# Hybrid Hyena / attention / RG-LRU block on one core: VectorE updates x first at the end of an FFN group, unused TensorE products at the norms and in the prologue

## The reference

```python
def rmsnorm(x, g):
    xf = x.astype(jnp.float32)
    y = xf * lax.rsqrt(jnp.mean(xf * xf, axis=-1, keepdims=True) + NORM_EPS)
    return (y * g.astype(jnp.float32)).astype(x.dtype)
...
def swiglu(h, w_in, w_out):
    gate, up = jnp.split(h @ w_in, 2, axis=-1)
    return (jax.nn.silu(gate) * up) @ w_out
...
    for i in range(DEPTH):
...
        m_lat = jnp.split((s_lat @ ada_w[i] + ada_b[i])[:, None, :], 6, axis=-1)
        m_ctx = jnp.split(s_ctx @ ada_w[i] + ada_b[i], 6, axis=-1)
        h_lat = modulate(rmsnorm(x_lat, norm1_g[i]), m_lat[0], m_lat[1])
        h_ctx = modulate(rmsnorm(x_ctx, norm1_g[i]), m_ctx[0], m_ctx[1])
...
        x_lat = x_lat + m_lat[2] * y_lat
        x_lat = x_lat + m_lat[5] * swiglu(modulate(rmsnorm(x_lat, norm2_g[i]), m_lat[3], m_lat[4]),
                                          ffn_w_in[i], ffn_w_out[i])
```

## Time and profile before

| | us |
|---|---|
| median of 3 runs | 3465.39 |
| lowest, highest | 3463.32, 3470.06 |
| the profiled execution | 3466.77 |
| its span, first to last instruction | 3465.0 |
| TensorE busy | 3201.0 |
| VectorE busy | 1670.7 |
| ScalarE busy | 939.8 |
| GpSimd busy | 350.0 |

### The profile page before, as it was taken

How to read it: one execution, slowest core, us unless ns; L and a number is a source line. 1 busy time by engine, 2 the same in 40 slices (tenths; PEclk the granted TensorE clock), 3 DMA queues, 4 the chain that set the end, 5 groups by cost and what they waited for, 6 DMA issues and landing times. The chain is left out here.

```text
span 3465.0 us, 39696 instructions
## 1 busy us (share of the span) xinstructions
PE 3201.0 (92%) x15846; PEld 2539.7 (73%) x15846; DVE 1670.7 (48%) x2146; ACT 939.8 (27%) x1205; POOL 350.0 (10%) x263
## 2 busy tenths in 40 slices
PE   6999997899766989999999999899969899999999
PEld 5788864555455778878888888678757788888887
DVE  5433237566687452444343444767774433333333
ACT  4222223344311231111111111377872311111111
POOL 1000000577422100000000000200001000000000
PEclk9999999799878989999999999999989999999999
DMA  4666610000312201111111111211113111111111
GB/s 188 224 224 207 200 42 1 0 1 9 124 73 85 97 31 37 37 41 38 36 36 36 36 36 38 75 40 37 38 33 115 49 49 43 48 48 48 48 48 73
DMA packets 65195, 231.63 MB, mean 67 GB/s; under 512 B 7911, under 2 KB 17511, under 8 KB 63560
## 3 DMA queue, kind: packets, MB, share of 16 engines
q1 hardware_dynamic: 50600, 199.26, 16.7%
q0 software_dynamic: 4000, 17.37, 1.4%
q10 hardware_dynamic: 10496, 13.63, 1.2%
HBM read 204.55 MB, written 25.69 MB: 66 GB/s over the span
## 5 line engine op out<-in xcount | busy, mean ns | idle before, releaser
L252 PE MATMUL bank<-h_pair,w_hi 128*128 128x512 f32 (+1 forms) x2448 | 620.1, 380 | 8.1 <-DVE h_pair L1849 7.2
L252 PEld LDWEIGHTS bank<-h_pair,w_hi 128*128 128x128 f32 x2448 | 442.3, 188 | 97.2 <-issue 8.9
L238 DVE TENSOR_TENSOR w_lo<-w_raw,w_hi 128x1024 fp32r<-128x1024 f32 x194 | 262.6, 1354 | 433.0 <-ACT w_hi L232 429.3
L268 PE MATMUL bank<-h_pair,w_hi 128*128 128x512 f32 x1344 | 366.8, 394 | 0.0
L252 PE MATMUL bank<-h_pair,w_lo 128*128 128x512 f32 (+1 forms) x1224 | 353.5, 379 | 0.0
L1781 DVE SCALAR_TENSOR_TENSOR x<-bank,c_mods,x 128x1024 f32<-128x1024 f32 (+3 forms) x280 | 273.0, 1007 | 143.5 <-PE bank L252 140.3
L232 ACT ACTIVATE w_hi<-w_raw 128x1024 fp32r<-128x1024 f32 x194 | 203.8, 1050 | 481.6 <-PE bank L268 238.5
L268 PEld LDWEIGHTS bank<-h_pair,w_hi 128*128 128x128 f32 x1344 | 227.9, 188 | 43.4
L252 PEld LDWEIGHTS bank<-h_pair,w_lo 128*128 128x128 f32 x1224 | 221.3, 188 | 44.0
L268 PE MATMUL bank<-h_pair,w_lo 128*128 128x512 f32 x672 | 208.3, 391 | 0.0
L276 DVE COPY ffn_part<-bank 128x256 f32<-128x256 f32 x42 | 17.8, 425 | 383.5 <-PE bank L268 383.5
(11 more groups left out here) (336 smaller groups left out, 5137.5 us busy)
## 6 DMA issues: line engine op xcount, KB each, us to landing
w_raw<-in_weights SPq DMA_DIRECT2D x194, 512.0 KB, 3.3
ada_late_w<-in_ada_w SPq DMA_DIRECT2D x80, 512.0 KB, 3.8
x<-in_x SPq DMA_DIRECT2D x2, 5120.0 KB, 15.7
h_gate<-u_scratch SPq DMA_DIRECT2D x4, 2560.0 KB, 9.3
ada_w<-in_ada_w SPq DMA_DIRECT2D x16, 512.0 KB, 17.4
u_scratch<-uc POOLq DMA_DIRECT2D x12, 640.0 KB, 5.1
spec_lat<-f_spec ACTq DMA_DIRECT2D x4, 1792.0 KB, 9.2
h_spec<-spec_lat SPq DMA_DIRECT2D x2, 3584.0 KB, 12.4
```

Of the source, the lines that this page charges most:

```text
L238: e.tensor_tensor(k.w_lo[s][:, :], k.w[s][:, :], k.w_hi[s][:, :].bitcast(F32), ALU.subtract).then_inc(k.split_lo[s], 1)
L252: mm = e.matmul(out[:, c:c + m], w[:, c1:c1 + P], x[:, c:c + m], start=(first and kk == 0 and n == 0), stop=(last and kk == kt - 1 and n = ...
L268: mm = e.matmul(out[:, c:c + m], w, x[:, half, c:c + m], start=(first and n == 0), stop=(last and n == 2))
```

## The change

In an FFN group VectorE no longer forms the low half of the second hidden tile and the `w_lo` of slot 1 before it updates x. The low half now stands behind x for m = 0, the `split_lo` of slot 1 behind x for m = 1. In the first group, which no take_out follows directly, the low half stays in its place.

Unused products (`spare`: ones times ident, float32, 128 by 128 by 128, written to an accumulator bank that nobody reads before it is written anew) are added: 20 at the end of `even_out`, `ffn(0)` and `rg_out`, behind a wait for x of tile m = 6; 10 behind the spreading of each of the three later norms; 36 in the prologue behind the filter's second layer. In the prologue ones and ident are loaded ahead of x, the first weight pair ahead of the last four adaLN tiles, and ScalarE splits that pair behind tiles 10 and 11.

```diff
+SPARE_FIRST, SPARE_AHEAD, SPARE_BEHIND = 36, 20, 10
+
+def spare(k, e, count, bank=0):
+    for _ in range(count):
+        e.matmul(k.bank[:, bank, 0:P], k.ones[:, :], k.ident[:, :], start=True, stop=True)
+
+def spare_ahead(k, e, ph):
+    e.wait_ge(k.acc_free[0], ph.a0 + ph.uses + 1)
+    spare(k, e, SPARE_AHEAD)
...
@@ Norm.tensor
         self.stats(k, e)
         self.spread(k, e)
+        spare(k, e, SPARE_BEHIND)
...
@@ prologue, sync
+            e.dma_start(k.ones[:, :], d["ones"]).then_inc(ones_landed, 16)
+            e.dma_start(k.ident[:, :], d["ident"]).then_inc(ones_landed, 16)
             e.dma_start(k.x[:, :, :], d["x"]).then_inc(x_landed, 16)
-            ada.load_first(k, e)
-            e.dma_start(k.ones[:, :], d["ones"]).then_inc(ones_landed, 16)
-            e.dma_start(k.ident[:, :], d["ident"]).then_inc(ones_landed, 16)
+            ada.load_first(k, e, 0, 12)
+            load_pair(k, e, w0)
+            ada.load_first(k, e, 12, ADA_FIRST)
             for name in names:
                 e.dma_start(k.c[name][:, :], d[name]).then_inc(others, 16)
-            load_pair(k, e, w0)
...
@@ prologue, tensor
             mm.then_inc(mm_full, 1)
+            e.wait_ge(ones_landed, 32)
+            spare(k, e, SPARE_FIRST, 7)
             e.wait_ge(silu_ready, 1)
...
                 if n == STATS_BEHIND:
-                    e.wait_ge(ones_landed, 32)
                     e.wait_ge(ss_ready, 1)
...
@@ prologue, scalar
-                if n >= ADA_FIRST - 2:
-                    s = n - (ADA_FIRST - 2)
+                if STATS_BEHIND < n <= STATS_BEHIND + 2:
+                    s = n - (STATS_BEHIND + 1)
                     split_hi(k, e, s, w0, k.acc_full[s], 1)
...
@@ even_out, ffn (if not last) and rg_out, tensor, at the end
+            spare_ahead(k, e, ph)
...
@@ ffn, vector
+            def low_half(g, buf, t):
+                e.wait_ge(hi_done, g * HG + (t + 1))
+                e.tensor_tensor(hid_lo[buf][:, t, 0:tokens], hid[:, 0:tokens],
+                                hid_hi[buf][:, t, 0:tokens].bitcast(F32), ALU.subtract).then_inc(lo_done, 1)
...
                     e.sem_inc(k.acc_free[1], 1)
-                    e.wait_ge(hi_done, g * HG + (t + 1))
-                    e.tensor_tensor(hid_lo[buf][:, t, 0:tokens], hid[:, 0:tokens],
-                                    hid_hi[buf][:, t, 0:tokens].bitcast(F32), ALU.subtract).then_inc(lo_done, 1)
+                    if first or t < HG - 1:
+                        low_half(g, buf, t)
...
                 for s in range(2):
                     e.wait_ge(k.acc_free[s], at[1] + 1)
-                split_lo(k, e, 1, at[0])
                 for m in range(KT):
+                    if m == 1 and not ends:
+                        low_half(g + 1, 1 - buf, HG - 1)
+                    if m == 2:
+                        split_lo(k, e, 1, at[0])
                     if m == half and not (ends and last):
                         split_lo(k, e, 0, at[0] + 1)
                     e.wait_ge(k.acc_full[m % 2], full(at[1] + m // 2))
```

More of the change, by code:

```diff
@@ L441, in turned, with load_first @@
         return k.bank[:, 3, 2 * n:2 * n + 2] if n < ADA_FIRST else k.bank[:, 6, 2 * P:2 * P + 2]
-    def load_first(self, k, e):
-        for n in range(ADA_FIRST):
+    def load_first(self, k, e, first, last):
+        for n in range(first, last):
             e.dma_start(self.first_w[n][:, :, :], k.d["ada_w"][n]).then_inc(self.landed[n // 4], 16)
@@ L1941, in _ @@
             schedule(e, take_in, take_out)
+            if not last:
+                spare_ahead(k, e, ph)
         @block.scalar
```

2 lines of the change are left out of this document (1 added, 1 removed).

## The result

The changed kernel takes 3424.55 us (median of 4 executions, 3423.64 to 3428.06) against 3466.47 us of the kernel before on the same chip (4 executions, 3463.32 to 3470.06): ratio 0.9881, 95% interval 0.9864 to 0.9898. That is 41.9 us less; 3423 was forecast. Its profiled execution took 3424.37 us, with a span of 3422.6.

What follows compares the result with a forecast made beforehand. TensorE's products, 92% of the span, plus its standstills and half-clock stretches were taken to bound the kernel. 29.5 - 0.4 + 11 + 2.5 = 42.6 us off 3465.4 gave 3423 us, with a range of 3410 to 3438 (0.85).

Steps and rivals of the forecast that it cites:

- the four terms: Whole kernel: FFN groups 29.5 us, last group of FFN 0 -0.4, norms 11, prologue 2.5.
- The FFN groups: Group ends of both FFNs: TensorE's waits for VectorE's x vanish, 10 x 1.95 and 10 x 1.0, 29.5 us.
- The rival of half the gain: FFN boundaries: another link, such as the low half waiting for ScalarE, holds x; gain 15 to 27 us; chance 0.05.
- bounds: FFN group ends: 25.4 us of waits, or 33.9 counted from weight loads, as the queue restarts earlier and first products are slower.
- The room of 1 us at every later step: FFN group end: each VectorE step after the reorder has 1 us or more to spare, so no other wait appears.
- The last group: Last group of FFN 0: the moved w_lo comes under a GpSimd sum of squares; -0.4 us, at most 2.0.
- The norms: Three norms between stages: unused products keep or bring back the clock for sums, spreading and first products; 9 to 16, taken 11 us.
- The prologue: Prologue: 0.9 us from higher clock and the sums' vanished wait, 1.6 from coefficients beginning earlier; together 2.5 us.
- The 0.9 for the clock and the sums: Prologue: adaLN tiles at higher clock less a late start, and no wait of the sums for ident; between -1 and 2.5 us.
- The clock holds in the prologue: Rival, prologue: adaLN tiles take 0.8 to 0.9 us, 8 to 10 us more gain, 3405 to 3413; chance 0.10.
- Slower: Rival: the 126 unused products reach the path, costing 126c - 33 us; slower by over 0.2% from c = 0.56; chance 0.03.
- Clock not held: Rival, norms and prologue: unused products partly at half clock, or clock lost in the sums; gain 27 to 37 us; chance 0.18.

Runs made afterwards that it cites:

- experiment 2: Changed kernel with only one VectorE move at FFN group ends: only the w_lo moved, 3433.09 us; only the low half moved, 3451.38 us.
- experiment 5: Changed kernel, last groups reordered: w_lo of slot 1 back ahead of x, 3421.76 us; also w_lo of slot 0 one tile later in FFN 0, 3418.01.
- experiment 4: Changed kernel without the 36 unused products of the prologue, moved loads and splits kept: 3421.56 us, ratio 0.9864 to the kernel before.
- experiment 3: Changed kernel with other unused products at the norms: forty ahead instead of twenty, 3434.13 us; only ten behind, 3430.23; only twenty ahead, 3425.18.
- experiment 6: Changed kernel with last group mended, without the prologue's 36, plus three unused products between each norm's sums and spreading: 3418.93 us.
- the mended kernel: Changed kernel with w_lo of slot 1 back ahead of x in last groups and w_lo of slot 0 one tile later in FFN 0: 3418.01 us.

## Why the prediction was right, and where it was not

The mechanisms held, but the total is nearer than its terms. Against the profiles the four terms missed by +1.7, -2.8, +1.0 and +0.7 us and a stage without a change by -0.7; these cancel to within 0.2, and that is luck.

*The FFN groups.* Right in kind and nearly in size: 31.2 us for 29.5. A boundary of FFN 0 gave 2.02 instead of 1.95 and one of FFN 1 1.1 instead of 1.0. The kernel with this part alone shows the same 31.2 us in its trace, less 1.9 in its last group, and is 27.9 us faster. The rival of half the gain is out. The measured 31.2 lies between the 25.4 and 33.9 taken as bounds, though the reason given for the upper one is misread: the weight loads show the longer waits because they end earlier, not because they restart earlier (both restart at 2068.42 behind the wait of the earlier trace rows). The working had a gap that the total hid: it set low half and w_lo in a row as VectorE's work alone, and the w_lo hung on ScalarE's w_hi (experiment 2). The room of 1 us at every later step was as forecast: no new wait at m = 3 or m = 4.

*The last group* is the term that was mis-sized: -0.4 forecast, -3.2 measured. The wait grew by 0.4, from 2.97 to 3.36, as worked out; the other 2.8 us are products at half the clock behind it (the trace with the same wait and the clock at 1.00 is 2.8 us shorter there, experiment 5). I took the price of a delay as its length, where the delay stands in front of work whose clock it can cost. But the unlengthened wait can lose the clock as well (three executions of five, experiment 5), and the profile of before happens to be one that kept it; so of the 3.2 us the change is shown to have caused 0.4, and whether it has any part in the rest is not shown. The 2.0 that I gave as the most did not hold it. By the Trainium skill, SBUF — State Buffer, "SBUF: two separate sides", VectorE with two SBUF inputs and a GpSimd instruction that reads SBUF exclude each other; the trace agrees in kind: the w_lo took 1.22 us alone, 2.23 and 3.59 beside GpSimd's sums, and those 3.51 where the undisturbed ones are 2.96.

*The norms.* 12.0 in the profile, 10.6 in the mean of seven, 11 forecast. The 10.6 are against the one profile of before, 152.1; three executions with the old norms lie at 152.1, 153.2 and 152.2, and against their mean the gain is 11.0. The price of an unused product was 0.23 (0.24 taken). Sums 2.36, 2.36 and 1.92 as forecast. That the clock mostly falls around the spreading and now and then holds is what happened, 4.8, 3.1 and 4.1 us; the granted clock at 1.00 between the stages, which I had named as a sign, showed at all three norms up to the end of the sums, and through the spreading at one. The first 15 products took 3.5, 3.7 and 3.9 us (forecast 3.4; before 5.4, 4.9 and 5.3). By the Trainium skill, TensorE: Matmul & The Clock Gate, Part 1, the moment of a clock change is not tied to the kernel's start; the traces agree, since the same norm code gave anything from 140.1 to 142.8 us over the three norms.

*The prologue.* 3.2 in the profile for 2.5 forecast, and 1.1 of the 3.2 is luck. Between the two profiles the spreading differs, with the next adaLN tile behind it; before, and with the change:

```profile
51.63 4.62 PE L349 MATMUL bank<-c_ident,c_rstd 128*128 128x128 f32 x20
56.18 0.76 PE L470 MATMUL bank<-ada_w,c_silu_c 128*32 128x128 f32 x16
```

```profile
51.30 3.47 PE L364 MATMUL bank<-c_ident,c_rstd 128*128 128x128 f32 x20
54.70 0.64 PE L485 MATMUL bank<-ada_w,c_silu_c 128*32 128x128 f32 x16
```

The clock came back at 56.5 and at 53.4. That is not the change: from the start of the spreading to the next tile it is 3.4 to 4.5 us with the old prologue (three executions) and with the new one (eleven). The code's own part is steady. From that tile to the first product of the stage it is 10.21 to 10.33 us in the three and 8.62 to 8.67 in the eleven: 1.6 us for the splits, as forecast. It has two pieces, ScalarE's copy of the last columns without a w_hi ahead of it (0.7), and the coefficients without the two w_lo (1.0). The 0.9 for the clock and the sums was 0.3: the 36 products took 9.7 us instead of 11.1 and did not make the adaLN products late, but what the clock won at the first two tiles went back in the next wait (experiment 4), and of the sums' wait of 0.60 about 0.3 came through: they begin at 42.45 on average instead of 42.78, while the adaLN products begin later with their transfer, at 26.9 instead of 26.3. In all the first product starts at 64.0 us on average over the eleven (63.3 to 64.7) and at 65.9 over the three (65.2 to 66.5): 1.9 us.

*The rivals.* The clock holds in the prologue: it fell 2.7 us into the adaLN products. Slower: 126 products at 0.23 us are 29.0, and 33 us lay idle; experiment 3 shows the price when there is no cover. Clock not held: the sums held it in every trace with the twenty, save one norm of experiment 6.

What stays open: why the clock falls over a wait of 3 us in some executions and not in others, and how much of the difference between kernels within 3 us is the kernel. The experiments show these as facts of single executions; nothing here sets the moment.

## What to carry to other kernels

Before moving one of two instructions that stand ahead of a late one, look for what each of them waits for on a third engine: a step that fills somebody's wait costs less than its duration, and the step behind it more. Unused products in a stretch in which TensorE is idle anyway pay where thin or short work follows; count them against the idle time, since the first one beyond it costs in full. They pay nothing where the work behind them soon waits for another engine's list, as in the prologue. Before a gain read from two profiles is put down to a change, look whether the same stretch differs as much between executions of the same code. And a stall of a few us ahead of TensorE's products can cost as much again in clock, so a stall at the end of a stage is worth a look even where the totals call it small.

## What the runs showed of the hardware

Executions of the same code fall into different clock histories far from any edit. In the attention, 12 products of 384 columns took 6.47 us in the changed kernel's profile and 4.14 in that of the mended kernel, with the granted clock at 0.50 and 1.00:

```profile
495.79 6.47 PE L1121 MATMUL bank<-wq,lat 128*128 128x384 f32 x12 [0.56 <-ACT qT L1165]
```

```profile
497.17 4.14 PE L1121 MATMUL bank<-wq,lat 128*128 128x384 f32 x12 [1.24 <-ACT qT L1165]
```

The three profiles with the new prologue whose first product stood at 63.3 to 63.5 all show the 6.4 us; those at 63.7 to 64.7 show the 4.14. From the first product to the last one ahead of FFN 0 the former take 1181.3 to 1181.5 us, the latter 1178.8 to 1179.5. So the executions that were ahead by up to 1 us in the prologue lost about 2 in the attention. This is larger than several of the terms that I summed, and it is the reason why 3421.8, 3424.6 and 3425.2 us are not told apart here.
